# Two of eight groups of modulation sums moved from FFN blocks into the start of the two mixers

## The chip, the cores and the metric

The kernel runs on one core of one Trainium2 chip. The metric is the device time of one execution, in microseconds (us), from launch to end; the profiler's span runs from the first to the last instruction. TensorE does the matmuls, VectorE (DVE) and ScalarE (ACT) the elementwise work, and SyncE (SP) issues the DMAs.

## The reference

Two layers of a transformer-like trunk are computed for 128 context tokens and 512 latent tokens at width 1024. The two token sets share all weights, but each has its own conditioning vector.

```python
mod = (silu(c) @ w_mod[l] + b_mod[l]).reshape(1, 1, 9, D_MODEL)   # c_ctx for the context tokens
x = x + 0.5 * mod[:, :, 2] * swiglu(modulated(0, x), ffn_w_in[l, 0], ffn_w_out[l, 0])
out = mixer(modulated(1, x))      # layer 0: gated MLP beside attention; layer 1: mLSTM beside a Fourier mixing
x = x + mod[:, :, 5] * out
x = x + 0.5 * mod[:, :, 8] * swiglu(modulated(2, x), ffn_w_in[l, 1], ffn_w_out[l, 1])
# modulated(j, y) = rmsnorm(y, g[j]) * (1 + mod[:, :, 3j + 1]) + mod[:, :, 3j]
```

`w_mod` is 2 x 1024 x 9216 numbers of 4 bytes. Its product with two vectors is small work for the engines but has to be streamed whole from memory.

## The kernel before

The program is written out by hand, one instruction list for each engine, with semaphores between them. The order of the whole is: FFN block 0, even mixer, FFN blocks 1 and 2, odd mixer, FFN block 3. All large products are split into high and low parts: ScalarE makes the high part of a weight tile (`split_hi`), VectorE the low part (`split_lo`), and TensorE multiplies hi x hi, lo x hi and hi x lo (`split_product`).

**The modulation.** The 18432 columns of `w_mod` are nine groups ("quads") of 2048. Group 0 is formed at the opening. Each of groups 1 to 8 is cut into 16 grains (half of the columns, one of 8 row tiles), of 524 KB each. SP loads a grain with two DMAs (`load_grain`) into one of three buffers `mod_grain`; grain g waits until grain g-3 is used (`mod_used`). TensorE forms it with four matmuls on 32 columns each (`mod_sums`), which the profile shows as eight records. When all 16 are in, ScalarE copies the sums to `quad_rows`, TensorE turns them (four matmuls against `pick_quad`), and VectorE adds the bias and keeps the result in `mod` (`keep_quad`, four small operations; after the first two it signals `quad_kept`). `QUADS` says which FFN block forms which group: block 0 forms 1, 2, 3, block 1 forms 4, 5, 6, block 2 forms 7 and 8. Inside a block the grains go in pairs after items 1, 3 and 5 of a double of hidden tiles (`GRAIN_STEPS`): the first group in doubles 1 to 3, the second in 4 to 6, the third in 7 to 9. Group 3 is the shift and scale of FFN block 1; group 8 the scale and gate of FFN block 3, so both are first read after a mixer.

**The start of a mixer.** The last FFN outputs are added to x in halves of 320 tokens, squared and summed. TensorE sums over partitions (`half_sums`), ScalarE takes the root (`root`), VectorE inverts, and TensorE spreads the inverse (`spread_inverse`). ScalarE then shifts and rounds one row tile after another (`high(kt, hf)`, in `mix_norm`), VectorE makes the low parts (`h_lo_ready`). In the middle of this ScalarE and VectorE split the weights of the mixer's second unit. The sums of the second half of tokens stand in TensorE's list at row tile 2 of the first unit, the spread of their inverse at row tile 3.

In the even mixer `fresh_token_units` runs three loops of eight row tiles: unit 0 on token tiles 0 and 1, unit 1 on the same, unit 0 on tiles 2 and 3; then the other tiles. In the odd mixer `fresh_pairs` runs four passes of 48 matmuls: first half of tokens with unit 0 and unit 1, second half with unit 0 and unit 1. The first half's sums go to banks 4, 0, 2, 6, the second half's to 5, 1, 3, 7. After the four passes the products of the gates follow.

ScalarE's list in the odd mixer after `mix_norm`:

```python
keep(0)      # waits for the end of feature tile 0: unit 0, second half
keep(1)
split(2)     # high parts of the third unit's weights
keep(2)
```

VectorE's list there is: low part of the gate weights, three memsets, a memset in `v_one` (which lies in the memory of `mod_grain`), `split(2)`, `split(3)`.

SP's list in the even mixer: units 0, 1, small loads, unit 2, then a wait for the end of unit 0, `rope` and two more loads, unit 3. In the odd mixer: units 0, 1, a wait for the end of the FFN block, six small loads (the largest `state_C`, 512 KB), units 2, 3.

## Time and profile before

| | us |
|---|---|
| median of three runs | 2452.64 |
| lowest and highest | 2449.16, 2453.02 |
| the profiled execution | 2447.98 |
| its span | 2446.2 |

TensorE is busy for 2385.3 us, VectorE for 1452.3, ScalarE for 980.2. The DMAs move 251.67 MB, 103 GB/s on the mean. In the profile, a line like L987 is the source line that issued an instruction; L987 is `split_product`, L1124 the matmul of `mod_sums`, L1135 the turn, L1257 the first product of `fresh_token_units`. "Idle before" an instruction is time in which its engine stood still; the name behind the arrow is what ended it. Matmuls overlap, so the distance from start to start is what one of them takes, not its own duration. The profile counts an engine as busy when any instruction of it is under way.

### The profile page before, as it was taken

The numbers are of one execution on the slowest core, as the hardware profiler recorded it, in microseconds if no ns is written. First come the engines' busy times: TensorE is split into PE (matmuls) and PEld (weight loads), VectorE is DVE, ScalarE is ACT, GpSimd is POOL, SyncE is SP. The second block draws the span as 40 slices with busy tenths as digits, with TensorE's granted clock in tenths as the row PEclk, the third lists the DMA queues.
The fourth block names the chain that finished last, engine by engine and source line by source line (L and its number), as shares of the span: only waits on it lengthen the run. The fifth ranks groups of instructions, "written<-read, shape, count | busy, mean of one in ns | idle before, by whom it ended". The sixth has DMA issues, their size and how long they took to land.

```text
span 2446.2 us, 40529 instructions
## 1 busy us (share of the span) xinstructions
PE 2385.3 (98%) x17084; PEld 2286.6 (93%) x17084; DVE 1452.3 (59%) x2197; ACT 980.2 (40%) x1542; POOL 0.2 (0%) x4
## 2 busy tenths in 40 slices
PE   6999999999989999999999999999999999999998
PEld 5999999989769899999998999999999999999998
DVE  4755645657766855645677456475334758567463
ACT  6432423344556433423464234144314355334242
POOL 0000000000000000000000000000000000000000
PEclk9999999999999999999999999999999999999999
DMA  7434443221102434544225343123221022222231
GB/s 278 149 119 130 155 155 117 84 81 57 54 18 78 156 112 130 165 145 130 87 78 181 114 156 112 57 90 92 85 70 57 6 70 70 91 65 88 68 95 70
DMA packets 251311, 251.67 MB, mean 103 GB/s; under 512 B 15010, under 2 KB 244346, under 8 KB 251130
## 3 DMA queue, kind: packets, MB, share of 16 engines
q1 hardware_dynamic: 251130, 249.08, 31.8%
q8 instruction: 135, 2.21, 0.4%
q14 instruction: 46, 0.38, 0.1%
HBM read 245.76 MB, written 3.28 MB: 102 GB/s over the span
## 4 chain that ended last, share of the span: by engine, by line
PE 88%; DVE 5%; ACT 3%; DMA 2%; issue 2%; SPq 0%; DVEq 0%; ACTq 0%
PE banks L987 75%; PE banks L1124 2%; DVE w_lo L2362 1%; DMA mod_grain<-w_mod 1%; PE banks L1297 1%; PE banks L1299 1%; PE banks L1298 1%; PE banks L1384 1%; PE banks L1396 1%; PE banks L1151 1%; ACT prob L2176 0%; PE banks L1411 0%; PE banks L1577 0%; DMA w_raw<-ffn_w_in 0%; DVE hid_lo L2607 0%
## 5 line engine op out<-in xcount | busy, mean ns | idle before, releaser
L987 PE MATMUL banks<-b_hi,w_hi 128*128 128x320 f32 x2496 | 783.7, 314 | 18.2 <-DVE b_lo L2513 7.5
L987 PE MATMUL banks<-b_hi,w_lo 128*128 128x320 f32 x2496 | 773.6, 310 | 0.0
L987 PE MATMUL banks<-b_lo,w_hi 128*128 128x320 f32 x2496 | 773.6, 310 | 0.0
L987 PEld LDWEIGHTS banks<-b_hi,w_hi 128*128 128x128 f32 x2496 | 470.9, 189 | 49.4 <-issue 33.8
L1818 ACT ACTIVATE w_hi<-w_raw 128x1024 fp32r<-128x1024 f32 x296 | 310.8, 1054 | 411.3 <-PE banks L987 282.1
L987 PEld LDWEIGHTS banks<-b_lo,w_hi 128*128 128x128 f32 x2496 | 471.2, 189 | 0.0
L987 PEld LDWEIGHTS banks<-b_hi,w_lo 128*128 128x128 f32 x2496 | 471.0, 189 | 0.0
L2362 DVE TENSOR_TENSOR w_lo<-w_raw,w_hi 128x1024 fp32r<-128x1024 f32 x296 | 361.5, 1223 | 169.6 <-ACT w_hi L1818 167.7
L987 PE MATMUL banks<-hid_hi,w_hi 128*128 128x320 f32 x1664 | 397.0, 311 | 1.6 <-DVE hid_lo L2937 1.4
L987 PE MATMUL banks<-hid_hi,w_lo 128*128 128x320 f32 x1664 | 394.7, 309 | 0.0
L987 PE MATMUL banks<-hid_lo,w_hi 128*128 128x320 f32 x1664 | 394.6, 309 | 0.0
L2390 DVE SCALAR_TENSOR_TENSOR x<-banks,mod,x 128x128 f32<-128x128 f32 x354 | 135.1, 434 | 339.3 <-PE banks L987 339.3
L987 PEld LDWEIGHTS banks<-hid_hi,w_hi 128*128 128x128 f32 x1664 | 282.6, 188 | 2.6 <-DVE hid_lo L2937 1.7
L987 PEld LDWEIGHTS banks<-hid_lo,w_hi 128*128 128x128 f32 x1664 | 282.6, 188 | 0.0
L987 PEld LDWEIGHTS banks<-hid_hi,w_lo 128*128 128x128 f32 x1664 | 282.5, 188 | 0.0
L2383 DVE TENSOR_TENSOR w_raw<-w_raw 128x1024 f32<-128x1024 f32 x160 | 195.3, 1221 | 11.1 <-DMA w_raw<-ffn_w_in 5.7
L1824 ACT ACTIVATE w_hi<-w_raw 128x1024 fp32r<-128x1024 f32 (+1 forms) x96 | 93.3, 984 | 232.6 <-PE banks L987 232.6
L1978 ACT ACTIVATE hid_hi<-work 128x640 fp32r<-128x640 f32 x88 | 64.2, 734 | 161.1 <-DVE work L2688 149.4
L2368 DVE TENSOR_TENSOR w_lo<-w_raw,w_hi 128x1024 fp32r<-128x1024 f32 (+1 forms) x96 | 107.8, 1134 | 11.7 <-ACT w_hi L1824 10.6
L2661 DVE TENSOR_TENSOR work<-work,banks 128x320 f32<-128x320 f32 x80 | 38.9, 487 | 117.9 <-ACT work L2007 117.9
L2007 ACT ACTIVATE work<-banks 128x320 f32<-128x320 f32 x80 | 35.0, 438 | 163.0 <-PE banks L987 163.0
L1807 ACT ACTIVATE w_hi<-w_raw 128x2048 fp32r<-128x2048 f32 (+1 forms) x26 | 48.0, 1846 | 103.0 <-PE banks L987 49.4
(319 smaller groups left out, 2497.4 us busy)
## 6 DMA issues: line engine op xcount, KB each, us to landing
w_raw<-ffn_w_in SPq DMA_DIRECT2D x176, 512.0 KB, 4.8
mod_grain<-w_mod SPq DMA_DIRECT2D x256, 256.0 KB, 5.3
w_raw<-ffn_w_out SPq DMA_DIRECT2D x64, 512.0 KB, 4.5
w_raw<-ffn_w_out SPq DMA_DIRECT2D x32, 384.0 KB, 3.5
w_raw<-w_in_odd SPq DMA_DIRECT2D x20, 512.0 KB, 4.7
mod_first<-w_mod SPq DMA_DIRECT2D x4, 2048.0 KB, 15.6
w_raw<-w_in_even SPq DMA_DIRECT2D x12, 512.0 KB, 5.0
w_raw<-w_out_even SPq DMA_DIRECT2D x8, 512.0 KB, 4.4
```

The lines of the kernel that those rows point to most:

```text
L987: ins = pe.matmul(o, w3[w], v3[v][cols], start=first and i == 0, stop=last and i == 2, skip_group_check=onto_read)
L1124: ins = pe.matmul(bank[MODB][j * MOD_ROWS:(j + 1) * MOD_ROWS, hf * GRAIN:(hf + 1) * GRAIN], wide_c[:, kt, :], mod_grain[:, g % GRAIN_BUFS, ...
L1807: act.activation(split_view(w_hi, kind, parity(unit)), raw_view(kind, parity(unit)), ACT.Copy).then_inc(hi_ready, 1)
L1818: act.activation(ring_in(w_hi, in_slot(d, t)), operand(d, t), ACT.Copy).then_inc(hi_ready, 1)
L1824: act.activation(ring_out(w_hi, out_slot(c, u), CHUNKS[c]), out_operand(c, u), ACT.Copy).then_inc(hi_ready, 1)
L1978: act.activation(hid_hi[:, k + s, :], work[:, s, 0:2, :].rearrange("p a b -> p (a b)"), ACT.Copy)\
L2007: act.activation(work[:, s, 1, :], role(d, s, "A"), ACT.Copy).then_inc(u2_kept, 1)
L2362: dve.tensor_tensor(ring_in(w_lo, q), operand(d, t), ring_in(w_hi, q).bitcast(F32), ALU.subtract).then_inc(lo_ready, 1)
L2368: dve.tensor_tensor(ring_out(w_lo, q, n), out_operand(c, u), ring_out(w_hi, q, n).bitcast(F32), ALU.subtract)\
L2383: dve.tensor_tensor(out_, in0, in1, op).then_inc(sums_done, 1)
L2390: ins = dve.scalar_tensor_tensor(out=xs, in0=bank[banks[hf]][:, in_bank], scalar=mod_col(v, layer, 3 * j + 2, d), in1=xs, op0=ALU.mult, op ...
L2661: dve.tensor_tensor(work[:, s, 1, :], work[:, s, 1, :], role(d, s, "C"), ALU.add).then_inc(c12_done, 1)
```

## The change

Groups 3 and 8 leave blocks 0 and 2. `QUADS` becomes ((1, 2), (4, 5, 6), (7,), ()). Their grains are formed in front of single row tiles of the mixers' first two units: `FRESH_GRAINS` gives the number for each of 16 steps, ten in unit 0 and six in unit 1. In the even mixer the sums stay in bank 4 and are turned after the third loop; VectorE keeps them before tile 6. In the odd mixer they lie in bank 3; they are turned inside the third pass, and the fourth pass, which writes bank 3, waits for `quad_kept`. VectorE's `keep_quad` and the memset of `v_one` go behind `split(2)` there. ScalarE copies the rows in `mix_norm` after row tile 5 of the second half. SP loads the grains between the mixer's own loads.

```diff
-QUADS = ((1, 2, 3), (4, 5, 6), (7, 8), ())
+QUADS = ((1, 2), (4, 5, 6), (7,), ())
+EVEN_QUAD, ODD_QUAD = 3, 8
+FRESH_GRAINS = (2, 1, 2, 1, 1, 1, 1, 1, 1, 1, 1, 1, 1, 1, 0, 0)
...
+        def quad_bank(quad):
+            return bank[3] if quad == ODD_QUAD else bank[MODB]
+        def fresh_grains(quad, step):
+            first = sum(FRESH_GRAINS[:step])
+            return [(quad, n) for n in range(first, first + FRESH_GRAINS[step])]
...
@@ even_sp
                     if i == 2:
+                        load_grains([(EVEN_QUAD, n) for n in range(GRAINS)])
                         sp.wait_ge(w_used, EU + 1)
@@ odd_sp
+                    if i == 2:
+                        load_grains([(ODD_QUAD, n) for n in range(9, GRAINS)])
                     if i == 1:
+                        load_grains([(ODD_QUAD, n) for n in range(GRAIN_BUFS)])
                         sp.wait_ge(w_used, OU)
...
                         sp.dma_start(state[:, :, :, 0:P], a["state_C"][0, 0].rearrange("d h e k -> e d h k"))\
                             .then_inc(odd_in, 16)
+                        load_grains([(ODD_QUAD, n) for n in range(GRAIN_BUFS, 9)])
@@ mod_sums
-                    if n == 0 and quad == QUADS[f][0]:
+                    if n == 0 and f is not None and quad == QUADS[f][0]:
                         pe.wait_ge(first_prod, 2 * f + 2)
@@ mod_step: the turn becomes a function, with quad_bank(quad) for bank[MODB]
+            def turn_quad(quad):
+                pe.wait_ge(quad_rows_ready, quad)
...
@@ fresh_token_units
                 for kt in range(KT):
+                    mod_sums(None, fresh_grains(EVEN_QUAD, kt))
                     if kt == 2:
                         half_sums(1, 1)
...
                 for kt in range(KT):
+                    mod_sums(None, fresh_grains(EVEN_QUAD, KT + kt))
                     for t in range(2):
                         products(1, t, kt, 2 + t)
...
+                turn_quad(EVEN_QUAD)
                 for fill, (u, t) in enumerate(FILLS[6:2 * TT], 6):
@@ fresh_pairs
+                            if hf == 1 and u == 1:
+                                pe.wait_ge(quad_kept, ODD_QUAD)
                             for kt in range(KT):
+                                if hf == 0:
+                                    mod_sums(None, fresh_grains(ODD_QUAD, KT * u + kt))
+                                elif u == 0 and kt == HK:
+                                    turn_quad(ODD_QUAD)
                                 if hf == 0 and u == 0 and kt == 2:
                                     half_sums(4, 1)
@@ mix_norm, ScalarE
                 for kt in range(KT):
                     high(kt, 1)
+                    if kt == 5:
+                        keep_quad_rows(EVEN_QUAD if n == MIX_NORMS[0] else ODD_QUAD)
...
+            def keep_quad_rows(quad):
+                act.wait_ge(mod_used, GRAINS * quad)
+                act.activation(quad_rows[:, :], quad_bank(quad)[:, :], ACT.Copy).then_inc(quad_rows_ready, 1)
@@ even_dve
-                for r in range(2, 7):
+                for r in range(2, 6):
                     even_keep(r)
+                keep_quad(EVEN_QUAD)
+                even_keep(6)
                 split(2)
@@ odd_dve
                 chain.inc(dve.memset(m_start[:, :], 0.0))
+                split(2)
+                keep_quad(ODD_QUAD)
                 chain.inc(dve.memset(v_one[:, :, :, P:P + 1], 1.0))
-                split(2)
                 split(3)
```

## Rows read from the trace of the kernel before

**Rows 1.** page, parts 1 and 4: busy time and share; chain that ended last

```profile
PE 2385.3 (98%) x17084; PEld 2286.6 (93%) x17084; DVE 1452.3 (59%) x2197; ACT 980.2 (40%) x1542; POOL 0.2 (0%) x4
...
PE 88%; DVE 5%; ACT 3%; DMA 2%; issue 2%; SPq 0%; DVEq 0%; ACTq 0%
```

**Rows 2.** order of time, TensorE, a step with two grains: start, us, what

```profile
390.39 1.07 PE L1124 MATMUL banks<-mod_grain,wide_c 128*32 128x256 f32 x16
391.39 0.42 PE L987 MATMUL banks<-b_hi,w_hi 128*128 128x320 f32 x1
...
399.62 0.42 PE L987 MATMUL banks<-b_hi,w_hi 128*128 128x320 f32 x1
```

**Rows 3.** order of time, TensorE, the turn of a group

```profile
153.16 0.95 PE L1135 MATMUL banks<-pick_quad,quad_rows 128*128 128x8 f32 x8
153.96 0.39 PE L987 MATMUL banks<-b_hi,w_hi 128*128 128x320 f32 x1
```

**Rows 4.** order of time, TensorE, even mixer; brackets: idle before, releaser

```profile
509.89 0.36 PE L1257 MATMUL banks<-w_hi,h_hi 128*128 128x256 f32 x1 [1.15 <-DVE h_lo L2480]
...
515.08 0.39 PE L1257 MATMUL banks<-w_hi,h_hi 128*128 128x256 f32 x1 [2.04 <-DVE h_lo L2480]
...
525.02 0.39 PE L1257 MATMUL banks<-w_hi,h_hi 128*128 128x256 f32 x1 [0.75 <-DVE w_lo L2355]
...
530.88 0.28 PE L1257 MATMUL banks<-w_hi,h_hi 128*128 128x256 f32 x1
```

**Rows 5.** order of time, ScalarE, even mixer

```profile
514.00 0.24 ACT L1848 ACTIVATE rms<-banks,eps 64x5 f32<-64x5 f32 x1
...
517.76 0.44 ACT L1854 ACTIVATE ss<-banks 128x320 f32<-128x320 f32 x1 [0.86 <-PE banks L1151]
```

**Rows 6.** TensorE at a late grain; requests and landings, the second 1295.6 to 1297

```profile
1297.49 0.64 PE L1124 MATMUL banks<-mod_grain,wide_c 128*32 128x256 f32 x8 [1.60 <-DMA mod_grain<-w_mod]
...
L816 SPq DMA_DIRECT2D mod_grain<-w_mod x2: 368/420/471, 1298.2 to 1298.6; - x2
...
DMA to landing us min/median/max: 3.0/3.1/3.2
...
DMA to landing us min/median/max: 3.7/3.9/4.1
```

**Rows 7.** order of time, TensorE, odd mixer

```profile
1700.99 0.39 PE L987 MATMUL banks<-h_hi,w_hi 128*128 128x320 f32 x1 [1.15 <-DVE h_lo L2480]
...
1716.30 0.41 PE L987 MATMUL banks<-h_hi,w_hi 128*128 128x320 f32 x1
...
1730.48 0.31 PE L987 MATMUL banks<-h_hi,w_hi 128*128 128x320 f32 x1
```

**Rows 8.** order of time, ScalarE, odd mixer

```profile
1705.10 0.24 ACT L1848 ACTIVATE rms<-banks,eps 64x5 f32<-64x5 f32 x1
...
1730.24 1.43 ACT L2210 ACTIVATE q_f<-banks 128x320 f32<-128x320 f32 x4 [7.73 <-PE banks L987]
1731.53 1.94 ACT L1807 ACTIVATE w_hi<-w_raw 128x2048 fp32r<-128x2048 f32 x1
```

**Rows 9.** order of time, VectorE, odd mixer; keeping of a group in a block

```profile
1733.49 2.29 DVE L2355 TENSOR_TENSOR w_lo<-w_raw,w_hi 128x2048 fp32r<-128x2048 f32 x1 [9.11 <-ACT w_hi L1807]
...
158.64 0.25 DVE L2429 TENSOR_TENSOR mod_tmp<-banks,mod_add 128x16 f32<-128x16 f32 x2
```

**Rows 10.** SP's first weight request after the odd mixer's small loads, and its landing

```profile
1703.04 3.00 SPq L862 DMA_DIRECT2D w_raw<-w_in_odd  x1
...
DMA to landing us min/median/max: 6.9/6.9/6.9
```

**Rows 11.** stretches: us, busy of each engine, granted clock, DMA share, GB/s

```profile
1293.00:1298.00 5.00, 3.40 (x32) 2.37 (x30) 3.17 (x4) 0.93 (x2) 0.00 (x0) 1.00 1.08 353
1705.00:1710.00 5.00, 3.83 (x20) 3.52 (x21) 2.87 (x5) 3.90 (x11) 0.00 (x0) 0.80 1.05 297
1710.00:1715.00 5.00, 5.00 (x21) 5.00 (x20) 3.01 (x4) 4.90 (x9) 0.00 (x0) 0.52 0.05 15
```

More of the change, by code:

```diff
@@ L1120, in mod_sums @@
                         pe.wait_ge(quad_kept, quad - 1)
-                    if n == 0 and quad == QUADS[f][0]:
+                    if n == 0 and f is not None and quad == QUADS[f][0]:
                         pe.wait_ge(first_prod, 2 * f + 2)
                     for j in range(QUAD):
-                        ins = pe.matmul(bank[MODB][j * MOD_ROWS:(j + 1) * MOD_ROWS, hf * GRAIN:(hf + 1) * GRAIN], wide_c[:, kt, :],
+                        ins = pe.matmul(quad_bank(quad)[j * MOD_ROWS:(j + 1) * MOD_ROWS, hf * GRAIN:(hf + 1) * GRAIN], wide_c[:, kt, :],
                                         mod_grain[:, g % GRAIN_BUFS, j, :], start=kt == 0, stop=kt == KT - 1)
@@ L1132, in mod_step @@
                 if quad is not None:
-                    pe.wait_ge(quad_rows_ready, quad)
-                    for m in range(MOD_TILES):
-                        ins = pe.matmul(bank[MODB][:, 2 * QUAD * m:2 * QUAD * (m + 1)], quad_rows[:, m * P:(m + 1) * P],
-                                        pick_quad[:, :, :].rearrange("p v j -> p (v j)"), start=True, stop=True)
-                    ins.then_inc(quad_turned, 1)
+                    turn_quad(quad)
+            def turn_quad(quad):
+                pe.wait_ge(quad_rows_ready, quad)
+                for m in range(MOD_TILES):
+                    ins = pe.matmul(quad_bank(quad)[:, 2 * QUAD * m:2 * QUAD * (m + 1)], quad_rows[:, m * P:(m + 1) * P],
+                                    pick_quad[:, :, :].rearrange("p v j -> p (v j)"), start=True, stop=True)
+                ins.then_inc(quad_turned, 1)
             def half_sums(n, hf):
@@ L2016, in rows @@
                     if quad is not None:
-                        act.wait_ge(mod_used, GRAINS * quad)
-                        act.activation(quad_rows[:, :], bank[MODB][:, :], ACT.Copy).then_inc(quad_rows_ready, 1)
+                        keep_quad_rows(quad)
                 for s in range(2):
@@ L2425, in keep_quad @@
                 dve.wait_ge(quad_turned, quad)
-                sums = bank[MODB][:, 0:MOD_TILES * 2 * QUAD].rearrange("p (m v j) -> p v j m", v=2, j=QUAD)
+                sums = quad_bank(quad)[:, 0:MOD_TILES * 2 * QUAD].rearrange("p (m v j) -> p v j m", v=2, j=QUAD)
                 first = QUAD * MOD_TILES * quad
```

## The prediction

> **What bounds the kernel now.** I read the page first, then the chain of waits, the time order of single engines around the two mixers, and the reloads of the grain buffers. TensorE carries 98% of the span and 88% of the chain that ended last; VectorE is at 59% and ScalarE at 40% [rows 1]. So a microsecond counts where TensorE spends it, or where it waits. The trace has two kinds of place. Inside an FFN block TensorE never waits in doubles 4 to 9: work taken from there is gained in full. At the start of a mixer it waits for the normalised activations, which ScalarE makes in a nearly unbroken row: it is idle 1.15 us before 509.89, 2.04 before 515.08 and 0.75 before 525.02 [rows 4], and in the odd mixer 1.15 before 1700.99 [rows 7]. There added work may be free. The question is whether sixteen grains fit into those holes.
>
> **What leaves the FFN blocks.** A step with two grains puts 16 matmul records between 390.39 and 391.39; from 391.39 to the same place after the next item is 8.23 us [rows 2], and the item's own 48 matmuls take 7.04 (two runs of 48 like them fill 1716.30 to 1730.48 [rows 7], with 0.1 for the start). A step costs 1.19 us: 1.0 for two grains and 0.19 for changing over. Eight steps are 9.5. The turn of a group takes 0.80 (153.16 to 153.96) and a change-over of 0.1: 0.9 [rows 3]. Each group gives back 10.4 us, both 20.8. Its 8.4 MB of transfers leave too; no wait of TensorE in those doubles was for a DMA, so that is worth nothing. ScalarE's copy and VectorE's four small operations lie beside matmuls: nothing.
>
> **What the mixers take on.** By the same rows one grain in a step of its own costs 0.5 + 0.19 = 0.69. The list of steps puts ten grains beside the first unit and six beside the second. Three buffers hold grains, so grain n+3 can be asked for only after grain n is used. The price of that is seen once where nothing else was queued: matmuls that end at 1297.49 + 0.64 = 1298.13, the request at 1298.19, its second half 0.47 later, and 3.1 more to land, 1301.8: 3.6 us. The grain before landed 3.9 after its request, by the same working 4.4 us [rows 6]. I take 4.1. The DMAs moved 353 GB/s at their fullest [rows 11], 1.5 us for the 524 KB of a grain.
>
> **Even mixer.** SP asks for the first three grains behind the third unit's weights, near 501, and they have landed when TensorE comes free at 508.7; two of them (1.19) fill the hole before 509.89. Step 2 wants grains 3 and 4 and stands ahead of the sums of the second half. Grain 0 is used at 509.3, so grain 3 lands near 513.4; grain 4, whose request goes behind it, near 514.4. The sums, which take 0.74, are done at 515.7. ScalarE took the root at 514.00 without having waited [rows 5]; it now goes 1.7 later. It had 0.86 of waiting before 517.76, which takes half of that up, so its chain, the weight split behind it, and unit 1's start at 525.02 move by 0.9. Unit 1 ran without a hole to 530.88 [rows 4], so its six grains are paid: 6 x 0.69 = 4.1. The buffer cycle there is 4.1 + 0.6 for three grains against TensorE's own 3 x (0.69 + 0.73) = 4.2, a step's products being an eighth of 525.02 to 530.88: 0.5 of waiting. The first two units end 0.9 + 4.1 + 0.5 = 5.5 later. ScalarE's copy of the rows (0.6) waits for the last grain in front of the two last activations; TensorE reaches those 4.3 us after it begins the third loop, so that is hidden. If this cover were gone it would be 2 us. The turn is paid again, 0.9; VectorE's keeping of it lies beside later tiles, where it was idle. SP stands behind the grains until about 530, but the next job in its queue, the rope load, waited for the end of unit 0's last tile anyway, and that lies behind the third loop. Even mixer: -10.4 + 5.5 + 0.9 = **-4.0**.
>
> **Odd mixer, supply.** Grains 0 to 2 land long before. Grain 3 stands behind six small transfers and the 512 KB state. In the kernel before the weights stood there: the first request, at 1703.04, held SP for 3.0 us and landed 6.9 later, at 1709.9 [rows 10]. A grain's two halves are as many bytes: 1709.7. Grain 4, 1.4 later, is used at 1711.6, and the sums are done at 1712.4. ScalarE took the root at 1705.10 [rows 8]: 7.3 later. As in the even mixer its wait for the spread inverse (0.86 there) takes about 1 of that up: the chain and unit 1's start at 1716.30 [rows 7] move by 6.3. Six grains add 4.1 and waiting for buffers 0.6. First half: +11.0, and the turn 0.9.
>
> **Odd mixer, the new wait.** The sums use bank 3, which unit 1's second half needs, so TensorE waits for quad_kept before it. VectorE keeps the group only behind split(2), the third unit's weights, and ScalarE makes their high parts only behind keep(0) and keep(1), which need the end of unit 0's second half. That end is at 1730.48, where TensorE went straight on [rows 7]. ScalarE's split began at 1731.53 and VectorE's at 1733.49, over at 1735.78: 5.3 after it [rows 8, 9]. Two operations of the keeping (0.25 together) and their hand-over make 0.5. TensorE stands still for **5.8 us**, with all the odd mixer's matmuls queued behind it; ScalarE and VectorE wait for those in turn, so nothing is won back. This is the largest single term of the odd mixer that no faster transfer removes.
>
> **Clock.** In the odd mixer's first unit the granted clock went from 0.80 in one stretch to 0.52, which is the lower level, 1.2 GHz, for most of it, and 20 matmuls then took 5 us [rows 11]; TensorE had stood idle in pieces shortly before. The change adds a wait of 6 us there and one of 5.8 with a dense pass behind it. 3.4 us at half rate on a full pass would cost 1.7, twice that 3.4. I take 1.7 after the second and 1.0 after the first, whose cost partly falls into waits. The Trainium skill, "TensorE: Matmul & The Clock Gate", section "What's actually happening", has the half rate as the default state, which activity lifts; the trace agrees (0.52 behind the idle pieces). By a reading of it in which the grains keep the engine active everywhere, these 2.7 us fall away.
>
> Odd mixer: -10.4 + 11.0 + 0.9 + 5.8 + 2.7 = **+10.0**. Both: -4.0 + 10.0 = **+6.0 us**.
>
> The Trainium skill, "DMA: Bandwidth & Descriptors", section "Anatomy of one DMA", fits 2.0 us plus bytes at 436 GB/s (for GpSimd's path), 2.6 for half a grain where the row has 3.1 to 3.9. By that figure, an estimate, the buffer cycle would be 3.2 and the sum about 1.5 lower. The rows decide.
>
> **Against what.** The profiled execution took 2447.98 us (span 2446.2); with +6.0, 2454.0. That execution lies 4.66 below the median of the runs, 2452.64; on the median the forecast is **2458.6 us**.
>
> **Bounds.** Supply costs at least nothing (grains on time): even -10.4 + 4.1 + 0.9 = -5.4, odd -10.4 + 4.1 + 0.9 + 5.8 = +0.4, together -5.0. At most: cycles of 5.5 us instead of 4.1 (five in a row, +7) partly in each mixer, say even +3 and odd +2, and 3 more for the clock: +14. Neither end leaves out the stall.
>
> **Rivals.**
> - *Grains on time* (faster). The transfers come early enough that no step waits and the root keeps its time. For it: the DMAs stood nearly empty in the odd mixer from 1710 to 1715, a share of 0.05 [rows 11]. Against: in the odd mixer grain 4 would have to land by 1703, before SP can even send grain 3. It gives -5.0, 2447.6; it decides once nearly all of the 7.3 us at the root is gone. Chance 0.13, half of it beyond the bound.
> - *The new wait doesn't bind.* If the third unit's split were done before unit 0's second half ends, the sum loses 5.8 and 1.7: -1.5, 2451.1. For it: ScalarE idled 7.73 us before keep(0) [rows 8]. Against: the weight buffer is unit 0's own, and its release is that very end. Chance 0.12.
> - *Starved and cold* (slower). Each three-buffer cycle takes 5 us or more, and the clock stays low through the passes behind both waits: +12, 2464.6. For it: 6.0 us without work ahead of step 2 in the odd mixer. Chance 0.20.
> - The forecast, 0.55.
>
> **From cases to numbers.** A measurement here tells about 0.2%, 4.9 us, from no change. Of the forecast's own spread (+1 to +10) some 0.6 lies above 4.9: 0.33, with the slow rival 0.53 slower. Half of the first rival and a trace of the forecast: 0.08 faster. The rest, 0.39, is within it. The range runs from 2449.6 (-3) to 2464.6 (+12).
>
> **What would show it.** After: doubles 7 to 9 of the first block and 4 to 6 of the third without L1124-type matmuls, 10.4 us shorter each; waits of TensorE for mod_grain at step 2 of both mixers, over 4 us in the odd one; ScalarE's second root about 1.7 and 7 us later against the mixer's start; a wait of 5 to 6 us for VectorE's keeping of the group ahead of the odd mixer's last first-pass quarter, and a granted clock of half behind it. The forecast is wrong if that last wait is missing, or if the odd root moves by less than 3 us.

## The result, and the profile after

The changed kernel takes **2469.72 us** (median of 4 runs, 2464.32 to 2469.91) against 2452.72 for the kernel before (4 runs, 2449.16 to 2453.02): ratio **1.0069**, 95% interval 1.0058 to 1.0081. It is 17.0 us slower; the forecast said 6.0 slower and reached to 12 at most. The profiled execution took 2469.90, its span 2468.1.

The page, parts 1, 4 and one group of part 5 (count, busy, mean ns, idle before):

```profile
PE 2393.4 (97%) x17084; PEld 2285.3 (93%) x17084; DVE 1451.8 (59%) x2197; ACT 981.1 (40%) x1542; POOL 0.2 (0%) x4
...
PE 86%; DVE 5%; DMA 3%; ACT 3%; issue 2%; SPq 1%; DVEq 0%; ACTq 0%
...
L1140 PE MATMUL banks<-mod_grain,wide_c 128*32 128x256 f32 x1024 | 76.0, 400 | 17.6 <-DMA mod_grain<-w_mod 17.5
```

The number of matmuls is that of [rows 1], but they are busy 8.1 us longer, and DMA went from 2% to 3% of the chain. The waits of TensorE (us in total, times, longest) name the new ones; the one for the grains was 4.5 us in 6 times before:

```profile
PE banks L1140 <- DMA mod_grain<-w_mod: 17.5, 16, 5.9
...
PE banks L1003 <- DVEq L2467: 5.4, 1, 5.4
```

Lines have moved: L1140 is a grain (L1124 before), L1164 the sums of the second half, L1171 the spread of their inverse, L1877 the root, L1883 the keeping of the inverse, L1003 `split_product`, L827 SP's load of a grain, L2467 the signal `quad_kept`. Even mixer, TensorE in order of time, beside [rows 4]:

```profile
507.32 0.64 PE L1140 MATMUL banks<-mod_grain,wide_c 128*32 128x256 f32 x8 [0.69 <-DMA mod_grain<-w_mod]
...
509.30 0.64 PE L1140 MATMUL banks<-mod_grain,wide_c 128*32 128x256 f32 x8 [1.34 <-DMA mod_grain<-w_mod]
509.87 0.74 PE L1164 MATMUL banks<-ones,ss 128*64 128x1 f32 x10
...
511.92 1.08 PE L1140 MATMUL banks<-mod_grain,wide_c 128*32 128x256 f32 x8
512.94 2.39 PE L1171 MATMUL banks<-ident,rms 64*128 64x64 f32 x10
```

Two short waits for grains 3 and 4 stand ahead of the sums. The forecast had grain 4 ready 1.0 us behind grain 3; their matmuls start 2.0 apart. Behind them the same eight matmuls of a grain take 1.08 instead of 0.64: the clock has fallen. ScalarE now waits for the sums and the spread:

```profile
510.65 0.26 ACT L1877 ACTIVATE rms<-banks,eps 64x5 f32<-64x5 f32 x1 [3.00 <-PE banks L1164]
...
515.37 0.44 ACT L1883 ACTIVATE ss<-banks 128x320 f32<-128x320 f32 x1 [1.79 <-PE banks L1171]
```

The mixer begins 6.6 us earlier in the span than before, so by [rows 5] the root is 3.25 later against the mixer's start and the inverse 4.2 later. In the odd mixer, which begins 6.2 earlier in the span, TensorE stands still for grain 3 until 1703.39 and the root is taken at 1707.16, 8.2 later by [rows 8]; the forecast had 7.3. The stretches of both mixers (columns as in [rows 11]):

```profile
505.00:510.00 5.00, 2.97 (x34) 1.38 (x33) 2.05 (x3) 2.59 (x6) 0.00 (x0) 1.00 0.86 272
510.00:515.00 5.00, 5.00 (x34) 3.95 (x34) 1.73 (x3) 2.86 (x7) 0.00 (x0) 0.58 0.76 239
515.00:520.00 5.00, 5.00 (x30) 3.25 (x29) 2.26 (x3) 4.57 (x8) 0.00 (x0) 0.50 0.37 113
...
1700.00:1705.00 5.00, 1.20 (x12) 0.32 (x16) 0.00 (x0) 0.00 (x0) 0.00 (x0) 0.71 1.07 331
1705.00:1710.00 5.00, 5.00 (x33) 3.03 (x33) 0.90 (x2) 2.78 (x7) 0.00 (x0) 0.50 0.75 234
1710.00:1715.00 5.00, 5.00 (x28) 3.93 (x24) 1.65 (x2) 2.65 (x7) 0.00 (x0) 0.50 0.71 212
...
1725.00:1730.00 5.00, 4.33 (x39) 2.60 (x39) 0.00 (x0) 0.00 (x0) 0.00 (x0) 1.00 0.96 292
```

0.50 is the lower level, 1.2 GHz. In each mixer it follows pieces of idle time (2.0 us of 505 to 510; 5.9 in one piece before 1703.4), and it stands while TensorE is busy without a break. It began at 510.8 in the even mixer, behind the two short waits, and at 1702.1 in the odd one, inside the long one. The chain that ended last in the odd mixer (start, us, what):

```profile
1700.32 4.52 DMA mod_grain<-w_mod
...
1704.88 1.08 PE banks L1140 x8
1705.96 1.16 PE banks L1164 x10
...
1720.75 0.37 SPq L827
1721.16 4.16 DMA mod_grain<-w_mod
1725.37 0.68 PE banks L1140 x8
1726.06 0.37 SPq L827
1726.47 4.64 DMA mod_grain<-w_mod
1731.15 0.64 PE banks L1140 x8
...
1743.58 1.80 ACT w_hi L1836
1745.40 2.29 DVE w_lo L2390
1747.69 0.18 DVE mod_tmp L2464 x2
1747.97 9.68 PE banks L1003 x48
```

Here the cycle of three grains can be read off: used 1725.37, asked 1726.06, landed and used 1731.15, 5.3 to 5.8 us for 1.57 MB. The last four lines are the new wait as forecast: split, low part, two small operations; then the fourth pass, which takes 9.7 us instead of 7.0, since half of it runs at the lower level.

Where the time went, matmul by matmul (the distance between the same two matmuls of the two lists, grains left out of the count):

| stretch | forecast | measured |
|---|---|---|
| FFN block 0 from 140 us on, group 3 taken out | -10.4 | -10.5 |
| even mixer, to unit 1's start | +0.9 | +7.0 |
| even mixer, unit 1 | +4.6 | +5.4 |
| even mixer, turn and third loop | +0.9 | +0.8 |
| FFN block 2, group 8 taken out | -10.4 | -10.6 |
| odd mixer, to unit 1's start | +6.3, clock +1.0 | +12.1 |
| odd mixer, unit 1 and turn | +5.6 | +5.9 |
| odd mixer, wait for `quad_kept` | +5.8 | +5.7 |
| odd mixer, fourth pass | +1.7 | +2.5 |
| sum | +6.0 | +18.3 |

The profiled execution differs from before's by 21.9. The other 3.6 are no work of the change's: 4.1 have arisen by 140 us, where the lists of the two kernels are still the same, and small differences of both signs arise in the blocks behind the mixers.

### The profile page after: what moved, and what is told of

Its sections match the earlier page's. It is cut to its first block, busy times and chain, and to the rows that moved or that the text cites. A ratio compares the mean times of both kernels' runs of the same rounds, so it can differ in the third digit from the quotient of the medians.

```text
span 2468.1 us, 40530 instructions
## 1 busy us (share of the span) xinstructions
PE 2393.4 (97%) x17084; PEld 2285.3 (93%) x17084; DVE 1451.8 (59%) x2197; ACT 981.1 (40%) x1542; POOL 0.2 (0%) x4
## 4 chain that ended last, share of the span: by engine, by line
PE 86%; DVE 5%; DMA 3%; ACT 3%; issue 2%; SPq 1%; DVEq 0%; ACTq 0%
PE banks L1003 73%; DMA mod_grain<-w_mod 2%; PE banks L1140 2%; DVE w_lo L2397 1%; PE banks L1320 1%; PE banks L1322 1%; PE banks L1321 1%; DMA w_raw<-ffn_w_in 1%; PE banks L1407 1%; PE banks L1419 1%; ACT w_hi L1847 1%; PE banks L1171 1%; ACT prob L2211 0%; DVE w_raw L2418 0%; ACT z_b L1890 0%
## 5 line engine op out<-in xcount | busy, mean ns | idle before, releaser
L1003 PE MATMUL banks<-b_hi,w_hi 128*128 128x320 f32 x2496 | 782.7, 314 | 20.6 <-DVE b_lo L2548 8.0
L1003 PE MATMUL banks<-b_hi,w_lo 128*128 128x320 f32 x2496 | 774.1, 310 | 0.0
L1003 PE MATMUL banks<-b_lo,w_hi 128*128 128x320 f32 x2496 | 774.1, 310 | 0.0
L1003 PEld LDWEIGHTS banks<-b_hi,w_hi 128*128 128x128 f32 x2496 | 471.4, 189 | 46.0 <-issue 29.9
L1003 PEld LDWEIGHTS banks<-b_lo,w_hi 128*128 128x128 f32 x2496 | 471.7, 189 | 0.0
L1003 PEld LDWEIGHTS banks<-b_hi,w_lo 128*128 128x128 f32 x2496 | 471.4, 189 | 0.0
L1003 PE MATMUL banks<-hid_hi,w_hi 128*128 128x320 f32 x1664 | 396.4, 310 | 1.6 <-DVE hid_lo L2974 1.4
L1003 PE MATMUL banks<-hid_lo,w_hi 128*128 128x320 f32 x1664 | 394.1, 309 | 0.0
L1003 PE MATMUL banks<-hid_hi,w_lo 128*128 128x320 f32 x1664 | 393.9, 309 | 0.0
L1003 PEld LDWEIGHTS banks<-hid_hi,w_hi 128*128 128x128 f32 x1664 | 281.9, 188 | 2.6 <-DVE hid_lo L2974 1.7
L1003 PEld LDWEIGHTS banks<-hid_hi,w_lo 128*128 128x128 f32 x1664 | 282.0, 188 | 0.0
L1003 PEld LDWEIGHTS banks<-hid_lo,w_hi 128*128 128x128 f32 x1664 | 282.0, 188 | 0.0
L2403 DVE TENSOR_TENSOR w_lo<-w_raw,w_hi 128x1024 fp32r<-128x1024 f32 (+1 forms) x96 | 107.9, 1134 | 11.7 <-ACT w_hi L1853 10.6
L1140 PE MATMUL banks<-mod_grain,wide_c 128*32 128x256 f32 x1024 | 76.0, 400 | 17.6 <-DMA mod_grain<-w_mod 17.5
```

Of the source, the lines that this page charges most:

```text
L1003: ins = pe.matmul(o, w3[w], v3[v][cols], start=first and i == 0, stop=last and i == 2, skip_group_check=onto_read)
L1140: ins = pe.matmul(quad_bank(quad)[j * MOD_ROWS:(j + 1) * MOD_ROWS, hf * GRAIN:(hf + 1) * GRAIN], wide_c[:, kt, :], mod_grain[:, g % GRAIN_ ...
L2403: dve.tensor_tensor(ring_out(w_lo, q, n), out_operand(c, u), ring_out(w_hi, q, n).bitcast(F32), ALU.subtract)\
```

## The experiments

Each kernel ran in five rounds beside the kernel before. "Even" and "odd" below are the extra time of the mixers' stretches in the profiled execution, counted as in the table above (even: to the end of the third loop; odd: to the end of the fourth pass). They come from one execution each, and the ratios from all. The even mixer's code is the same in "changed kernel", "keep first", "state late" and "even mixer alone", and took 13.2, 9.2, 13.1 and 12.3: differences of this size between two rows need not be the edit's.

| kernel | ratio, 95% interval | even | odd |
|---|---|---|---|
| changed kernel | 1.0069 [1.0058, 1.0081] | 13.2 | 26.1 |
| keep first | 1.0034 [1.0023, 1.0045] | 9.2 | 21.3 |
| sums first | 1.0058 [1.0046, 1.0070] | 10.5 | 26.8 |
| keep and sums first | 1.0038 [1.0025, 1.0051] | 10.9 | 21.8 |
| even mixer alone | 0.9994 [0.9985, 1.0003] | 12.3 | - |
| odd mixer alone | 1.0062 [1.0045, 1.0078] | - | 27.1 |
| no reload | 0.9984 [0.9973, 0.9995] | 5.2 | 13.2 |
| no reload, keep first | 0.9955 [0.9941, 0.9970] | 5.2 | 5.6 |
| half the bytes | 1.0027 [1.0017, 1.0036] | 5.3 | 23.8 |
| added matmuls | 1.0046 [1.0033, 1.0059] | 10.9 | 25.3 |
| both, spread out | 1.0056 [1.0041, 1.0070] | 15.1 | 19.7 |
| keep first, state late | 1.0038 [1.0025, 1.0051] | 13.1 | 20.2 |
| six grains, even alone | 0.9982 [0.9974, 0.9991] | 3.3 | - |

**One half of the change at a time.** Group 8, then group 3, back in its block.

```diff
-QUADS = ((1, 2), (4, 5, 6), (7,), ())
+QUADS = ((1, 2), (4, 5, 6), (7, 8), ())      # even mixer alone
+QUADS = ((1, 2, 3), (4, 5, 6), (7,), ())     # odd mixer alone
```

> Only group 3 goes to the even mixer; group 8 stays in block 2 as before the change. By the ledger of the two traces (10.5 us given back by the block, 13.2 taken by the mixer) the time is 2.7 us over before, ratio 1.001. By the prediction's sum (-10.4 + 6.4) it would be 4.0 us under it, 0.9984.

> Only group 8 goes to the odd mixer; group 3 stays in block 0. By the ledger of the traces (10.6 us given back, 25.8 taken) 15 us over before, ratio 1.006. By the prediction's sum 10 us over, 1.004. If the two moves hurt each other, this and the even one do not add up to the changed kernel's 17.

The even half measured 2450.29, ratio 0.9994: no change that can be told, where the forecast's own sum (-4.0) would be 0.9984, just below the interval, and the 1.001 expected from the profiled stretches lies above it; the median execution seems to pay less for the even mixer than the 12.3 of the profiled one. The odd half alone is 1.0062, +15 us against +10.0. The loss is the odd mixer's. The two halves add up to 1.0056, which the intervals allow beside the whole's 1.0069.

**Keeping group 8 ahead of the third unit's split.** `quad_kept` then comes before unit 0's second half ends.

```diff
-                split(2)
                 keep_quad(ODD_QUAD)
                 chain.inc(dve.memset(v_one[:, :, :, P:P + 1], 1.0))
+                split(2)
```

> The changed kernel with VectorE's keeping of group 8 (and the memset behind it) ahead of split(2) in the odd mixer. My reading of the new wait: TensorE's 5.4 us in front of the fourth pass go, and the pass runs in 7.0 us instead of 9.7, because the clock no longer falls behind a wait: 8 us less than the changed kernel, near 2461.7 us or 1.0035 of before. Rival 1, the wait only moves (TensorE then waits for the same work at split(2)'s weights): less than 2 us gained. Rival 2, the low clock there has nothing to do with the wait: 5.4 us gained and the pass still takes 9.7.

Ratio 1.0034, some 8.5 us under the changed kernel. The wait is gone and the fourth pass takes 7.0 again: 5.7 + 2.5 of the table. This pair is order alone, no bytes and no matmul. But the profiled odd mixer shows only 4.8 of it (21.3 against 26.1): a grain of unit 1 landed 6.7 us after its request, TensorE waited 2.5 for it, and 3.4 us at the lower level followed; whether that belongs to the edit is open. The other 4.0 between the two profiled executions are the even mixer's, whose code is the same. Two more pairs below differ in this edit alone: with the sums first it is worth 4.9 us by the ratios (1.0058 and 1.0038), without reloads 7.1 (0.9984 and 0.9955).

**The sums ahead of the grains.** In steps 2 and 3 of both mixers the sums and the spread go in front of the grains.

```diff
-                    mod_sums(None, fresh_grains(EVEN_QUAD, kt))
                     if kt == 2:
                         half_sums(1, 1)
                     elif kt == HK - 1:
                         spread_inverse(1, 1)
+                    mod_sums(None, fresh_grains(EVEN_QUAD, kt))
```

> The changed kernel with the sums of the second half of tokens (step 2) and the spread of their inverse (step 3) ahead of those steps' grains in both mixers; all grains and waits stay. Order theory: ScalarE's root keeps its time, its chain is no longer 4.2 (even) and 7 to 8 us (odd) late, and since that chain paced unit 1's start, the time falls by 8 us or more, near 1.003 of before. Supply theory: TensorE stands still for the grains in any case, and unit 1 begins when its ten grains are in; the root is early but unit 1's start moves by less than 2 us, and the ratio stays at 1.006 or more.

> The changed kernel with both repairs, keep_quad ahead of split(2) and the sums ahead of the grains. If they add: 8.6 us for the first, and for the second 8 (order theory, 1.000) or under 2 (supply theory, 1.003).

1.0058, an interval that overlaps that of the changed kernel. In the odd mixer unit 1 begins no earlier (13.9 us late instead of 12.1): TensorE takes its list in order, so products behind the grains of step 2 wait all the same, only the root doesn't. Behind grain 4, used at 1700.00, the clock was back at 1.00 from 1703.3 on, and TensorE then stood still 3.9 us for grain 9. In the chain that ended last:

```profile
1707.60 7.29 DMA mod_grain<-w_mod
...
1714.94 1.08 PE banks L1140 x8
```

Its request stands in SP's queue behind the third unit's weights, 1 MB. It landed 26.8 us after TensorE began the block's last matmul, and in the changed kernel, where TensorE came to it later, 26.6. So in the odd mixer a shorter stretch at half rate didn't bring unit 1 forward. With the early keeping the ratio is 1.0038, no better than the keeping alone. That the root is late is not what costs.

**No reload: the cost of supply.** Of groups 3 and 8 only the first three grains are loaded; the other 13 are formed from what the three buffers hold, so that part of the result is left out. Matmuls and order stay.

```diff
+                if quad in (EVEN_QUAD, ODD_QUAD) and n >= GRAIN_BUFS:
+                    return
```

> Leaves out part of the work: of groups 3 and 8 only the first three grains are loaded, and the other thirteen read the same three buffers again, so every matmul stays and no grain is waited for. If the supply of grains is the root (waits of 3.9 and 7.5 us, and the low clock that follows them), the ten grains beside unit 0 cost nearly nothing: even mixer +5, odd mixer +5 and the wait for quad_kept with its low clock +8, against 20.8 given back: about 3 us under before, 2450 us, and the half-rate stretches at both mixers' starts are no longer than before the change (6.8 us). If the order is the root (grains in front of the sums at steps 2 and 3), the root goes only 1 us later, and most of the loss stays with TensorE: at least 2458. If the low clock comes from the mixers' own idle times, it stays at 10 us or more and the time at about 2460.

> Both costs taken away at once: only the first three grains of groups 3 and 8 are loaded (the others are formed from the same buffers, so that part of the result is left out), and VectorE keeps group 8 before the third unit's split. What stays is the matmuls of the grains. The kernel without reloads came 3.9 us under the kernel before with a 5.7 us wait for quad_kept and a slow fourth pass behind it (2.2): if these costs add, 2443.5, ratio 0.997 (0.996 to 0.998); no wait of TensorE for quad_kept or for mod_grain. If the early keeping only moves the wait to somewhere else, 2447 to 2449 (0.998 to 0.999).

Without reloads the change is a gain: 0.9984, and with the early keeping 0.9955, 9.0 us faster than before. So the 26 grains loaded inside the mixers, with all that follows from waiting for them, cost 0.0085 of 2452, 21 us. In the profiled executions 8.0 of it lie in the even mixer, about half of that at the lower level, which the same code doesn't always meet, and 12.9 in the odd one. The stretches of the second kernel, both mixers:

```profile
505.00:510.00 5.00, 4.68 (x53) 3.40 (x53) 1.96 (x4) 3.99 (x11) 0.00 (x0) 1.00 0.00 0
510.00:515.00 5.00, 5.00 (x48) 3.32 (x47) 3.10 (x5) 4.94 (x9) 0.00 (x0) 1.00 0.01 3
...
1690.00:1695.00 5.00, 4.18 (x35) 3.26 (x33) 2.83 (x5) 3.86 (x11) 0.00 (x0) 1.00 1.06 297
1700.00:1705.00 5.00, 5.00 (x47) 3.19 (x50) 4.31 (x5) 4.84 (x11) 0.00 (x0) 1.00 0.52 157
```

In neither mixer does the clock fall, where it fell in both of the kernel before (0.67 from 515 to 520; the odd one in [rows 11]). Grains that are there fill the holes, and TensorE keeps the full rate. What stays, 5.2 and 5.6 us, is the bare price of 16 grains and a turn; the forecast's terms for it were 4.1 + 0.9.

**Half the bytes: rate or delay?** Every request, buffer, wait and matmul stays, but each load brings half of its columns; the other half is formed from what the buffer held, so that part of the result is left out.

```diff
-  mod_grain[:, g % GRAIN_BUFS, 2 * part:2 * part + 2, :], src[:, :, hf * GRAIN:(hf + 1) * GRAIN])
+  mod_grain[:, g % GRAIN_BUFS, 2 * part:2 * part + 2, 0:cols], src[:, :, hf * GRAIN:hf * GRAIN + cols])
```

> The changed kernel, but of each grain of groups 3 and 8 only half the bytes are loaded (256 of 512 columns in each of the four blocks); number of requests, buffers, waits and matmuls stay. The other half of the columns is formed from what the buffer held, so that part of the result is left out. Theory A, the rate of the DMAs: three grains are 1.57 MB, 5.3 us at the 295 GB/s that the stretches show while TensorE waits, so half the bytes should bring a cycle of three grains below TensorE's own 4.2 us: no waits for mod_grain in unit 1 of either mixer, the even mixer within 1 us of the kernel without reloads (+5.2 there), and all in all 2452 to 2456 (ratio 1.000 to 1.0015; the wait behind the state of the odd mixer stays at 4 us or more). Theory B, a fixed delay for each request and landing: cycles of 4.5 us or more stay, waits for mod_grain stay at 10 us or more of 17.5, time 2463 or more (1.0045).

1.0027 [1.0017, 1.0036]: above the 1.000 to 1.0015 of the theory of the rate, and below the 1.0045 of the theory of the delay. The waits are those that the rate foretold, of the whole span and of 1670 to 1800 (lines stand one further on in this kernel):

```profile
PE banks L1141 <- DMA mod_grain<-w_mod: 10.0, 5, 5.7
...
PE banks L1141 <- DMA mod_grain<-w_mod: 5.7, 1, 5.7
PE banks L1004 <- DVEq L2468: 5.4, 1, 5.4
```

The even mixer costs 5.3, the same as without any reload (5.2); in the odd one all waits for grains are gone but the first, which is as long as before, 5.7 us. So there are two costs of supply. One is bytes: in unit 1 a round of the three buffers takes 5.3 to 5.8 us, where TensorE's own work between the same two grains is 4.2, as forecast. (For the whole stream the sum is less clear: the 13 grains that are asked for after the mixer has begun are 6.8 MB, 23 us at the 292 GB/s of the stretch from 1725; from 508.7 to step 13, at 525.02 + 5 x 0.73 = 528.7, the kernel before had 20 us, and the matmuls of the 13 grains add 9.) The other is grain 3 of the odd mixer, which halving the grains' bytes doesn't bring forward: this kernel pays 23.8 there, against 13.2 without reloads, and that wait and the lower level that begins in it (17.1 us) make the difference, which lies in the first unit (11.7 late against 1.0).

**What the odd mixer's first wait is made of.** SP's requests there, in the changed kernel:

```profile
1696.25 0.58 SPq L935 DMA_DIRECT2D state<-state_C  x1
1696.88 14.10 SPq L827 DMA_DIRECT2D mod_grain<-w_mod  x12
```

The experiment asks for grains 3 to 8 ahead of the masks, the state n and the state C.

```diff
+                        load_grains([(ODD_QUAD, n) for n in range(GRAIN_BUFS, 9)])
                         sp.dma_start(masks[:, :, :], a["masks"].rearrange("m s t -> s m t")).then_inc(odd_in, 16)
...
-                        load_grains([(ODD_QUAD, n) for n in range(GRAIN_BUFS, 9)])
```

> The changed kernel with the early keeping of group 8, and in the odd mixer SP asks for grains 3 to 8 of group 8 ahead of the 256 KB of masks, the state n and the 512 KB of state C instead of behind them. Theory A (the first and longest wait for a grain there, 6.0 us in the kernel with the early keeping alone, is these 768 KB and their requests standing in front of grain 3): the wait falls by 2 to 3 us, the stretch at half the clock behind it shortens, and the time falls by 3 to 5 us under that kernel's ratio of 1.0034, to 1.0015 to 1.002. Theory B (the grains' own transfer, from the use of grain 0 on, is what is waited for): the wait stays above 5 us and the ratio at 1.003 or more. Because the same bytes have to pass later, some of the gain may come back as waits in the second unit; then 1.0025.

SP's requests, TensorE at grain 3, and the stretch behind it:

```profile
1692.65 13.44 SPq L827 DMA_DIRECT2D mod_grain<-w_mod  x12
```

```profile
1698.50 0.64 PE L1140 MATMUL banks<-mod_grain,wide_c 128*32 128x256 f32 x8 [3.56 <-DMA mod_grain<-w_mod]
```

```profile
1700.00:1705.00 5.00, 5.00 (x32) 3.11 (x32) 0.90 (x2) 2.66 (x7) 0.00 (x0) 0.50 0.75 240
```

The wait falls from 6.0 to 3.6, so 768 KB in front were 2.4 us of it. But the time stays: 1.0038 against 1.0034. 3.6 us of standing still were followed by the lower level too, and grain 9, the next in the chain that ended last, is late as before:

```profile
1711.12 7.47 DMA mod_grain<-w_mod
...
1718.64 0.64 PE banks L1140 x8
```

7.5 us to land, against 4.5 with the early keeping alone. The moved bytes stand in front of it now, but they are not the main of it: it took 7.3 us in the kernel with the sums first too, with only the third unit's weights ahead. In both, its request went out earlier. It landed 27.8 us after the block's last matmul began, against 27.0 with the early keeping alone. The odd mixer gains 1.1 in all (20.2 against 21.3), and not in its first unit. The even mixer's 13.1 against 9.2 is the same code; what differs there is the clock (below).

**Added matmuls: is it the standing still?** In front of step 2's grains TensorE does 12 (even) and 38 (odd) matmuls whose result nobody uses.

```diff
+                for _ in range(count):
+                    pe.matmul(bank[5][:, 0:HALF], w_hi[:, slot, 0, :], h_hi[:, 0, 0:HALF], start=True, stop=True)
```

> Adds work that is of no use: ahead of step 2's grains TensorE multiplies into an unused bank, 12 matmuls of 320 columns (1.8 us) in the even mixer and 38 (5.6 us) in the odd one, about as long as it stood still there; the outputs are unchanged. If the low clock follows the standing still, the stretches of 10.2 and 13.7 us at half rate shrink or go, and the steps behind, which took twice as long, give back 3 us or more in each mixer in spite of the added work: 1.005 or less. If supply alone paces the steps, or the low clock has another cause, the time is that of the changed kernel, 1.0069, or up to 2 us more.

1.0046: more work, and 5.6 us less time than the changed kernel. In the odd mixer the 38 matmuls (L1147; L1169 are the sums here) stand where the wait was:

```profile
1691.49 5.74 PE L1147 MATMUL banks<-h_hi,w_hi 128*128 128x320 f32 x38
...
1697.73 0.64 PE L1140 MATMUL banks<-mod_grain,wide_c 128*32 128x256 f32 x8 [0.51 <-DMA mod_grain<-w_mod]
...
1699.58 0.64 PE L1140 MATMUL banks<-mod_grain,wide_c 128*32 128x256 f32 x8 [1.21 <-DMA mod_grain<-w_mod]
1700.14 0.74 PE L1169 MATMUL banks<-ones,ss 128*64 128x1 f32 x10
```

Grains and sums run at 0.64 and 0.74 there instead of 1.08 and 1.23; the fall comes later, behind the next short waits. The stretches at the lower level are 3.4 and 10.2 us long, where they were 10.2 and 13.7. The gain of the whole run is larger than the odd stretch shows (25.3 against 26.1), and part of it is the even mixer (10.9 against 13.2), so it supports the clock's part without measuring it. Unit 1 of the odd mixer begins as late as without them (12.2 and 12.1): grain 9 is used 26.7 us after the block's last matmul in both.

**Where the grains stand.** Early keeping, sums first, and no grain in steps 2 and 3.

```diff
-FRESH_GRAINS = (2, 1, 2, 1, 1, 1, 1, 1, 1, 1, 1, 1, 1, 1, 0, 0)
+FRESH_GRAINS = (2, 1, 0, 0, 1, 2, 1, 1, 1, 1, 1, 2, 1, 2, 0, 0)
```

> The changed kernel with the early keeping of group 8 and the second half's sums ahead of the grains, and with no grain in steps 2 and 3: 2, 1, 0, 0, 1, 2, 1, 1, 1, 1, 1, 2, 1, 2 grains instead of 2, 1, 2, 1, 1, ... So the root and the spread of its inverse have nothing to wait for. Theory A (sixteen grains are 28 us of DMA at 295 GB/s and the first two units are shorter than that, so where the grains stand is of little weight): within 3 us of the same kernel with the old steps (2461.5), ratio 1.0025 to 1.005. Theory B (what costs is that the grains stand ahead of the sums and the spread): 5 us or more less, ratio 1.0015 or below.

1.0056, a little above the 1.0025 to 1.005 of the first theory and far from the second: grains that are used later free their buffers later, and the bytes are asked for later. The wait moves (16.4 us in 17 times), it doesn't go.

**Fewer grains.** The last six of group 3 in the even mixer, the sums first, and group 8 whole in its block.

```diff
+IN_BLOCK = 10
-FRESH_GRAINS = (2, 1, 2, 1, 1, 1, 1, 1, 1, 1, 1, 1, 1, 1, 0, 0)
+FRESH_GRAINS = (2, 1, 0, 0, 1, 1, 1, 0, 0, 0, 0, 0, 0, 0, 0, 0)
```

> A version meant to gain, from what the runs so far show: only the last six of group 3's sixteen grains go to the even mixer, three of them (which have landed) in front of row tiles 0 and 1, three in front of tiles 4, 5 and 6, none beside unit 1, with the sums ahead of them; group 8 stays in block 2. Block 0 gives back three steps, 3.6 us; the turn is paid once as before. If the mixer's holes take the six grains for nothing, 0.9985 of before. If one pass of three buffers is already too slow, or grains at half rate cost double, the mixer takes all of it back and the ratio is 1.000 or more.

0.9982 [0.9974, 0.9991], 2448.62 against 2450.97: the one whole kernel here that is below the kernel before. No matmul of the even mixer waits for a grain, though the clock fell there as it did before the change (0.50 from 515 to 520). Three steps and the turn fewer in the block give 4.4, the mixer takes 3.3: -1.1 in the profiled execution, where the ratio says -2.2 to -6.4. Both have the same sign; the rest of the size stays open.

## Why the forecast was wrong in size

The direction held, and so did the mechanism of most terms. What the block gives back (10.4, measured 10.5 and 10.6), the bare grains and turns (5.0, measured 5.2 and 5.6), the wait for `quad_kept` (5.8, measured 5.7) and the low clock in the fourth pass (1.7, measured 2.5) are right or nearly so. **The step that failed is the delay of unit 1's start in both mixers, the sum's term for unit 0: "its chain, the weight split behind it, and unit 1's start at 525.02 move by 0.9", and 6.3 + 1.0 in the odd one.** They measured 7.0 and 12.1. Together that is 10.9 of the 12.3 us between the two sums. The forecast let ScalarE's chain alone set that start, with the grains behind the sums costing nothing; what the runs show is TensorE paced by grains and by its clock. It has three parts.

- *The cycle of the buffers was too short.* I took 4.1 us for request and landing from a place where little else was queued [rows 6], 4.7 with TensorE's share; it is 5.3 to 5.8. I looked at the delay of one grain and not at the rate: three grains are 1.57 MB, which at 292 GB/s are 5.4 us. The full stretch of [rows 11] has 353 GB/s, and even that is 4.5. Grain 4 was put 1.0 behind grain 3, less than the 1.5 us that the forecast itself has for a grain; it was 2.0. The Trainium skill, "DMA: Bandwidth & Descriptors", section "Anatomy of one DMA", fits 436 GB/s behind a fixed delay for GpSimd's path; for these loads from SP the trace doesn't reach it, and the measurement decides. In the even mixer supply costs unit 0 2.0 us and unit 1 2.0, read from the kernel with the early keeping (2.6 and 5.8, at the full clock) against the one without reloads (0.65 and 3.8).
- *The clock was put on the wrong wait.* I charged 1.7 to the fourth pass, 1.0 to the odd mixer's start and nothing to the even mixer. The same instructions of the even mixer ran in one profiled execution at the full rate (keep first: unit 1 begins 2.6 late) and in three with a stretch at half (changed kernel 7.0, state late 6.6, even mixer alone 6.0): **3.4 to 4.4 us that go with the clock**, with nothing else changed there. That is the larger part of the even mixer's miss, and the same code doesn't always pay it. That it shows in full fits with the grains having filled the slack: in the kernel before, half rate stood in the even mixer too (6.8 us from 516.7 on), and TensorE still had 0.75 to wait before unit 1 [rows 4]. The Trainium skill, "TensorE: Matmul & The Clock Gate", section "What's actually happening", has the half rate as the default, which activity lifts. The traces agree in this: 0.50 in or behind every wait of 3.6 us and more for a grain or for `quad_kept` in these kernels, and 1.00 through both mixers of the kernel without reloads and with the early keeping. With six grains no grain was late, but the mixer's own waits were there and the clock fell.
- *The odd mixer's first wait was right, and what stands behind it was missing.* Grain 3 was put at 1709.7, which is 1703.5 with the mixer beginning 6.2 us earlier; measured 1703.39. The root was 8.2 late, for 7.3. But unit 1 began 12.1 late. Half the bytes leave 11.7, with 17.1 us at the lower level. The sums first, with 6.8 us at the lower level ahead of grain 9 instead of 13.7, give 13.9: TensorE waited 3.9 us for grain 9, behind the third unit's weights, which the forecast had nowhere. So with either of the two made smaller the other kept unit 1 about as late, and no run divides the 12.1 between them.

The forecast also read no wait for a DMA in the doubles that lose their grains; there was one, 0.27 us at 314.51. It changes nothing.

Of the rivals "starved and cold" named what came; its price, +12, was 5 too low. It speaks of the stall in the odd mixer and of the passes behind, and names nothing for unit 0 of the even one. "Grains on time" gave -5.0: the kernel without reloads measured -3.9 (0.9984), so its price was nearly right and its condition false. "The new wait doesn't bind" was priced at 5.8 + 1.7 = 7.5; taking the wait away gave 8.5, 4.9 and 7.1 in three pairs of kernels.

What stays open: why identical code keeps the full rate in one execution of the even mixer and not in the next (the waits for grains 3 and 4 ahead of it were 1.7 and 2.0 us together); what the odd mixer would do with grain 9 in time and the clock full, since no kernel with all its loads had both; and whether a fourth buffer would help, which no run tried.

## What to carry to other kernels

Before moving streamed work into a hole, divide the bytes of one round of its buffers by the rate that the profile shows when the DMAs are full, and compare that with the consumer's own work for the round; the delay of a single transfer says too little. Here a round took 5.3 to 5.8 us against 4.2. Then go through the whole queue that the loads stand in: the odd mixer's grain 3 stood behind 768 KB, and its grain 9 behind 1 MB of weights. The version that paid moved six grains of sixteen, three of which had landed. A hole that is filled with work that can itself be late is no longer slack: each wait in it counts, and so does the half clock behind it.

## What the runs showed of the hardware

- In the changed kernel 13.7 us at the lower level began inside the wait of 5.9 us, 6.8 inside that of 5.4, and 10.2 behind the two short ones of the even mixer (0.7 and 1.3), and stood on while TensorE was busy: a grain's matmuls took 1.08 us instead of 0.64, the spread 2.39 instead of 1.32.
- The same code of the even mixer ran through at 1.00 in one profiled execution and with 6.8, 10.2 and 10.2 us at the lower level in three others.
- With its holes filled by matmuls whose data were there, TensorE kept 1.00 through both mixers, which the kernel before didn't (0.67 and 0.52 in its stretches). The mean clock of the span was 0.995 instead of 0.992.
- Useless matmuls, 38 in place of a 6 us wait and 12 in the even mixer, made the kernel 5.6 us faster.
- Loads of 256 KB in pairs, three pairs under way at most, with two weight loads of 512 KB among them, moved 282 to 292 GB/s in the stretches from 1715 to 1730, and 331 from 1700 to 1705 beside the state; the median of the grain loads from request to landing was 3.9 us between 1685 and 1735.
- A grain's last load took 4.3 us to land when it was asked for 4.2 us after 1 MB of weights (changed kernel), and 7.3 us when it was asked for 1.1 us after them (sums first).
